# A residual update shared by two engines, and a first unit that multiplies rounded halves first

## The reference

```python
h = rms_norm(x, g_pre)          # x * rsqrt(mean(x*x) + 1e-6) * gain
m = branch(h)                   # starts with a product h @ W
x = x + rms_norm(m, g_post)     # in the second block 0.5 * for the two feed-forwards
```

## Time and profile before

| | |
|---|---|
| median of 3 runs | 3150.82 us (3149.11 to 3152.02) |
| the profiled execution | 3147.1 us, its span 3145.3 us |
| TensorE matmul busy | 2929.5 us, 93% of the span |
| TensorE weight load busy | 2289.0 us |
| VectorE busy | 1164.5 us |
| ScalarE busy | 1288.0 us |
| GpSimd busy | 1156.5 us |
| mean granted TensorE clock | 0.97 of full |

### The profile page before, as it was taken

One profiled execution on the slowest core, in us unless ns is written; L12 is line 12 of the kernel. 1 busy time (PEld: TensorE's weight loads), 2 busy tenths in 40 slices (PEclk: granted clock), 3 DMA queues, 4 the chain that ended last, 5 costly groups with the idle time before them and its releaser, 6 DMA issues.

```text
span 3145.3 us, 40673 instructions
## 1 busy us (share of the span) xinstructions
PE 2929.5 (93%) x14437; PEld 2289.0 (73%) x14437; DVE 1164.5 (37%) x1551; ACT 1288.0 (41%) x1707; POOL 1156.5 (37%) x256
## 2 busy tenths in 40 slices
PE   7998998999989989998999989999498999999997
PEld 5864686888768755886887768887296778678886
DVE  5154214555132362125553054430304531354422
ACT  5356443555235366434553233322224353333332
POOL 2410253344544200542445524455131325434453
PEclk9999998999999999999999989999699999999998
DMA  6210132233335100332332323322221213323322
GB/s 147 86 30 1 40 104 83 80 93 88 89 91 110 54 2 3 98 101 67 98 102 74 103 74 98 95 83 75 73 86 32 71 41 96 101 67 93 98 83 73
DMA packets 441756, 242.34 MB, mean 77 GB/s; under 512 B 39158, under 2 KB 440246, under 8 KB 441654
## 3 DMA queue, kind: packets, MB, share of 16 engines
q1 hardware_dynamic: 438320, 240.13, 27.6%
q10 hardware_dynamic: 3334, 0.85, 0.2%
HBM read 238.48 MB, written 2.70 MB: 77 GB/s over the span
## 4 chain that ended last, share of the span: by engine, by line
PE 60%; issue 27%; POOL 6%; DVE 3%; ACT 2%; DVEq 1%; SPq 1%; POOLq 0%; DMA 0%; ACTq 0%
PE pair L1459 54%; POOL wlo L454 6%; SPq L405 1%; PE pair L1641 1%; DVEq L970 1%; PE pair L1662 1%; DVE x L972 0%; ACT bP L775 0%; PE pair L1679 0%; PE pair L1721 0%; DVE nstat L1155 0%; DVE pair L968 0%; DVEq L973 0%; PE pair L1719 0%; PE pair L1877 0%
## 5 line engine op out<-in xcount | busy, mean ns | idle before, releaser
L454 POOL TENSOR_TENSOR wlo<-raw,whi 128x2048 fp32r<-128x2048 f32 x251 | 1156.2, 4606 | 1955.1 <-ACT whi L469 1955.1
L1459 PE MATMUL pair<-hh,whi 128*128 128x512 f32 (+1 forms) x2256 | 885.9, 393 | 35.4 <-DVE hl L944 23.0
L1459 PE MATMUL pair<-hl,whi 128*128 128x512 f32 (+1 forms) x2256 | 883.0, 391 | 0.0
L1459 PE MATMUL pair<-hh,wlo 128*128 128x512 f32 (+1 forms) x2256 | 882.8, 391 | 0.0
L469 ACT ACTIVATE whi<-raw 128x2048 fp32r<-128x2048 f32 x251 | 480.0, 1913 | 512.2 <-PE pair L1459 462.7
L1459 PEld LDWEIGHTS pair<-hh,whi 128*128 128x128 f32 (+1 forms) x2256 | 425.4, 189 | 135.8 <-DVE hl L944 22.8
L1459 PEld LDWEIGHTS pair<-hl,whi 128*128 128x128 f32 (+1 forms) x2256 | 425.5, 189 | 90.1
L1459 PEld LDWEIGHTS pair<-hh,wlo 128*128 128x128 f32 (+1 forms) x2256 | 425.0, 188 | 90.7
L1270 DVE TENSOR_TENSOR a2lo<-tmp,a2hi 128x512 f32 x44 | 200.0, 4546 | 79.5 <-ACT a2hi L760 79.5
L983 DVE COPY branch<-pair 128x512 f32 x32 | 22.1, 692 | 463.9 <-ACT sq L515 358.9
L1459 PE MATMUL pair<-a1hi,whi 128*128 128x512 f32 x352 | 139.7, 397 | 3.6 <-DVE a1lo L1248 3.6
(11 more groups left out here) (307 smaller groups left out, 3852.1 us busy)
## 6 DMA issues: line engine op xcount, KB each, us to landing
raw<-in_w_in SPq DMA_DIRECT2D x122, 512.0 KB, 4.1
raw<-in_w_up SPq DMA_DIRECT2D x88, 512.0 KB, 4.8
raw<-in_ffn_w_gate SPq DMA_DIRECT2D x44, 512.0 KB, 4.0
raw<-in_ffn_w_up SPq DMA_DIRECT2D x44, 512.0 KB, 5.2
raw<-in_w_out SPq DMA_DIRECT2D x24, 512.0 KB, 4.4
raw<-in_w_down SPq DMA_DIRECT2D x32, 384.0 KB, 3.6
raw<-in_ffn_w_down SPq DMA_DIRECT2D x32, 384.0 KB, 3.6
raw<-in_w_down SPq DMA_DIRECT2D x32, 320.0 KB, 4.0
```

What stands on the lines that cost most here:

```text
L454: pool.tensor_tensor(wlo[:, s, :], raw[:, s, :], whi[:, s, :].bitcast(f32), ALU.subtract).then_inc(lo_ready, 1)
L1459: o = pe.matmul(out, l, r, start=start and first, stop=stop and last)
```

## The change

Three things, in all handovers:

- **Residual update.** `post_norm` writes the normalised odd tile into `tmp` (SBUF) and the even one into PSUM. VectorE adds the even one to x, as a plain sum, and GpSimd adds the odd one (`odd_tiles`). The factor 0.5 is multiplied into the gains of norms 9 and 13 once, at the start. The semaphores are `t_odd`, `x_odd` and `x_even`; ScalarE squares the tiles in the order 1, 0, 3, 2, 5, 4, 7, 6.
- **Remainders.** In `pre_norm` odd tiles go to `tmp` too, and GpSimd makes their `hl` (`odd_remainders`); VectorE makes the even ones.
- **First unit.** A `ready` unit issues, for each k, whi x hh and wlo x hh for both banks after a wait for `hh`, then whi x hl for both banks after a wait for `hl`.

GpSimd's single loop over units is cut into loops with these pieces between them. SyncE waits for the eight sums of squares (`sq_used`) where it waited for `x_ready`. The first norm of the program keeps its form on VectorE.

```diff
+            def odd_tiles(j):
+                for c in range(4):
+                    pool.wait_ge(S.t_odd, 4 * j + c + 1)
+                    pool.tensor_tensor(x[:, 2 * c + 1], x[:, 2 * c + 1], tmp[:, c % 2], ALU.add).then_inc(S.x_odd, 1)
+            def odd_remainders(m):
+                for c in range(4):
+                    k = 2 * c + 1
+                    pool.wait_ge(S.hh_ready, KT * m + k + 1)
+                    pool.tensor_tensor(hl[:, k], tmp[:, c % 2], hh[:, k].bitcast(f32), ALU.subtract).then_inc(S.h_odd, 1)
...
+                rest(v0 + 16, 0)
+                odd_tiles(2 * l)
+                rest(v0 + 16, 1)
+                odd_remainders(2 * l + 1)
...
                 for k in range(KT):
-                    if k > 0:
+                    if k % 2 and k > 4:
+                        dve.wait_ge(S.h_odd, 4 * m + k // 2 - 1)
+                    dve.scalar_tensor_tensor(tmp[:, k // 2 % 2] if k % 2 else NORM[k // 2 % 2][:, :], x[:, k], gains[:, bass.ds(KT * n + k, 1)], RSTD[:, :],
+                                             ALU.mult, ALU.mult).then_inc(S.h_set, 1)
+                    if k % 2:
                         dve.drain()
-                    dve.scalar_tensor_tensor(NORM[k % 2][:, :], x[:, k], gains[:, bass.ds(KT * n + k, 1)], RSTD[:, :],
-                                             ALU.mult, ALU.mult).then_inc(S.h_set, 1)
-                    if k >= 1:
                         lower(k - 1)
-                lower(KT - 1)
...
-                for k0 in range(0, KT, 2):
-                    for k in (k0, k0 + 1):
-                        dve.scalar_tensor_tensor(NORM[k % 2][:, :], branch[:, k], gains[:, bass.ds(KT * n + k, 1)], RSTD[:, :],
-                                                 ALU.mult, ALU.mult)
+                def even(c):
+                    dve.tensor_tensor(x[:, 2 * c], NORM[c % 2][:, :], x[:, 2 * c], ALU.add).then_inc(S.x_even, 1)
+
+                for c in range(4):
+                    if c >= 2:
+                        dve.wait_ge(S.x_odd, 4 * j + c - 1)
+                    for k, to in ((2 * c + 1, tmp[:, c % 2]), (2 * c, NORM[c % 2][:, :])):
+                        o = dve.scalar_tensor_tensor(to, branch[:, k], gains[:, bass.ds(KT * n + k, 1)], RSTD[:, :], ALU.mult, ALU.mult)
+                        if k % 2 == 1:
+                            o.then_inc(S.t_odd, 1)
                     dve.drain()
-                    for k in (k0, k0 + 1):
-                        dve.scalar_tensor_tensor(x[:, k], NORM[k % 2][:, :], scale, x[:, k], ALU.mult, ALU.add).then_inc(S.x_ready, 1)
-                    dve.drain()
+                    even(c)
...
-                        ready(ki)
+                        ready[0](ki)
                         for b, _, c0 in tiles:
-                            wt = [w[s][:, k * width + c0:k * width + c0 + P] for w in (wh, wl)]
-                            o = three(bank[b][:, :], wt, [inp[0][:, ki], inp[1][:, ki]], j == 0, j == nk - 1)
+                            at = k * width + c0
+                            pe.matmul(bank[b][:, :], wh[s][:, at:at + P], inp[0][:, ki], start=j == 0, stop=False)
+                            pe.matmul(bank[b][:, :], wl[s][:, at:at + P], inp[0][:, ki], start=False, stop=False)
+                        ready[1](ki)
+                        for b, _, c0 in tiles:
+                            at = k * width + c0
+                            o = pe.matmul(bank[b][:, :], wh[s][:, at:at + P], inp[1][:, ki], start=False, stop=j == nk - 1)
```

More of the change, by code:

```diff
@@ L284, in build @@
             start_x gains_t gains_set tables_t tables_copied ang_ready sin_done tables_ready negones_set
-            x_ready sq_done sq_used sum_done rstd_done h_set hh_ready h_ready
+            x_ready x_even t_odd x_odd sq_done sq_used sum_done rstd_done h_set hh_ready h_even h_odd
             rs_ready rope_done k_exchanged cmp_in kvAB_ready v_ready v_ready_dve gateT_set gate_t gate_ready
@@ L371, in _ @@
                 unit(v0 + 2, 0, twin(W, 896, W, 1152, 0))
-                sp.wait_ge(S.x_ready, KT * (2 * l + 1))
+                sp.wait_ge(S.x_ready, KT)
+                sp.wait_ge(S.sq_used, KT * 4 * l + KT)
                 sp.wait_ge(S.tables_ready, 1)
@@ L485, in root, with pre_squares @@
                 act.activation(RSTD[:, :], RSTD[:, :], ACT.Exp, scale=-0.5).then_inc(S.rstd_done, 1)
[L487 to L492, removed]
+            def pre_squares(n, m, first=False):
+                for p in range(KT):
+                    k = p ^ 1
+                    if first:
+                        act.wait_ge(S.x_ready, k + 1)
+                    else:
+                        act.wait_ge((S.x_even, S.x_odd)[k % 2], 4 * (m - 1) + k // 2 + 1)
+                    if p >= 2:
+                        act.wait_ge(S.sq_used, KT * n + p - 1)
+                    act.activation(sq[:, p % 2], x[:, k], ACT.Square).then_inc(S.sq_done, 1)
                 root(n, True)
@@ L499, in pre_upper @@
                     act.wait_ge(S.h_set, KT * m + k + 1)
-                    act.activation(hh[:, k], NORM[k % 2][:, :], ACT.Copy).then_inc(S.hh_ready, 1)
+                    act.activation(hh[:, k], tmp[:, k // 2 % 2] if k % 2 and between is None else NORM[(k if between is not None else k // 2) % 2][:, :], ACT.Copy).then_inc(S.hh_ready, 1)
             def pre_norm(n, m):
@@ L1025, in _ @@
             dve.wait_ge(S.gains_t, 1)
-            dve.tensor_copy(gains[:, :], bank[6][:, 0:GAINS * KT]).then_inc(S.gains_set, 1)
+            dve.tensor_copy(gains[:, :], bank[6][:, 0:GAINS * KT])
+            dve.drain()
+            for n in (9, 13):
+                dve.tensor_scalar(gains[:, KT * n:KT * n + KT], gains[:, KT * n:KT * n + KT], 0.5, None, ALU.mult)
+            dve.drain().then_inc(S.gains_set, 1)
             dve.wait_ge(S.pos_in, 16)
@@ L1052, in _, with first_lower @@
             reduced(ang, 0.25, TWO_PI / 4)
-            pre_norm(0, 0)
+            dve.drain()
+            dve.wait_ge(S.rstd_done, 1)
+            def first_lower(k):
+                dve.wait_ge(S.hh_ready, k + 1)
+                dve.tensor_tensor(hl[:, k], NORM[k % 2][:, :], hh[:, k].bitcast(f32), ALU.subtract).then_inc((S.h_even, S.h_odd)[k % 2], 1)
+            for k in range(KT):
+                if k > 0:
+                    dve.drain()
+                dve.scalar_tensor_tensor(NORM[k % 2][:, :], x[:, k], gains[:, k:k + 1], RSTD[:, :], ALU.mult, ALU.mult).then_inc(S.h_set, 1)
+                if k >= 1:
+                    first_lower(k - 1)
+            first_lower(KT - 1)
             dve.wait_ge(S.sin_done, 2)
@@ L1759, in _ @@
                 for i in range(4):
-                    two_tiles(v0 + 14 + i // 2, i % 2, (yhi, ylo), (lambda k: pe.wait_ge(S.y_ready, 8 * l + k + 1)) if i == 0 else None)
+                    two_tiles(v0 + 14 + i // 2, i % 2, (yhi, ylo), y_tiles(8 * l) if i == 0 else None)
                 variance(4 * l + 1)
```

59 lines of the change are left out of this document (44 added, 15 removed).

## The result

| | before | after |
|---|---|---|
| median | 3150.34 us (4 runs, 3149.11 to 3152.02) | 3126.25 us (4 runs, 3122.07 to 3130.53) |
| ratio, with its 95% interval | | 0.9918, 0.9905 to 0.9931 |
| profiled execution, its span | 3147.1, 3145.3 us | 3122.07, 3120.3 us |
| GpSimd busy | 1156.5 us | 1222.2 us |

The kernel is 24 us faster by the medians, 25 by the two profiled executions, where I had predicted 18.1. Direction and places were right; the gain is larger than the forecast.

A forecast was written before the change was run, and what follows sets the result against it. TensorE was taken as the bound, standing still 3.9 us at each of six handovers. Squares 8.0 + first product 5.6 + clock 2 + end 2.9 - start 0.4 = 18.1 us off, giving 3132.7; own range 3128 to 3139, stretched to 3125 to 3142.

The forecast's parts named there:

- Squares, 8.0: Residual update in six handovers: x ready earlier, TensorE's squares end sooner without gaps; 8.0 us saved, bounds 5 and 10.
- First product, 5.6: After each handover's squares: TensorE starts on `hh` without waiting for `hl`; 0.93 us, six times, 5.6 us saved.
- GpSimd's piece, 1.2: One 512-column sum or subtraction on GpSimd in a handover takes 1.2 us.
- VectorE's pair, 2.15: Two tiles on VectorE in the residual update, two products and one sum, take 2.15 us.
- Two engines at SBUF, nothing: VectorE's new handover instructions have one SBUF and one PSUM tensor, so GpSimd does not hold them up; no cost.
- the slack that I gave the piece: Residual update: with d per GpSimd piece, last odd x comes at 0.8 + 4d, later than before from d = 2.7.
- Order of the halves, nothing: 47 units with new order and second wait per k keep pace 0.2265; no cost, upper bound 17.8 us.
- The clock, 2: Windows after the six handovers: shorter idle time gives back 2 us of 12.0 lost to lower clock; bounds -1 and 12.
- the clock stays up: Rival, behind the handovers: clock stays up after the shorter idle stretch, 10 us more, 3123; chance 0.06.
- End, 2.9: Kernel's end: the last tiles are transposed earlier, 2.9 us saved.
- Start, -0.4: Kernel's start: two tiny products and two drains before `gains_set`, four steps at 0.1, 0.4 us lost.
- its 3197 for a piece of 4.53 us: Rival "Slower", residual update: large fixed GpSimd cost, last odd x 7.2 later, seven times, some 3197; chance 0.03.

The follow-up runs named there:

- a second profile: The changed kernel run again with no edit, which gave a second profile; 3125.97 us, ratio 0.9924 to the kernel before.
- the order alone: Kernel before with only the first unit's new order and its two waits; update and remainders stay on VectorE; 3143.94 us, 0.9972.
- fill: Matmuls of a 128-column constant that keep TensorE busy, results overwritten; in both idle stretches of the changed kernel: 3124.52 us, 0.9917.
- fill_squares: Such filler matmuls in the idle time ahead of the squares; alone on the changed kernel 3121.7 us, with the start mended 3123.85 us.
- fill_product: Such filler matmuls between squares and first product; alone on the changed kernel 3128.93 us, on the kernel before 3151.95 us.

## Why the forecast was right, and where it fell short

**Squares, 8.0: right.** 7.9, 9.1 and 8.0 in the three profiles. TensorE ends this stretch, and it runs without gaps.

**First product, 5.6: right**, 5.3 with a second profile at 5.2; the order alone gives 5.3. TensorE does not run dry after it, and only because GpSimd helps: with VectorE alone it does, for 8.9 us.

**GpSimd's piece, 1.2: right**, 1.26 to 1.29; VectorE's pair, 2.15: 2.10. **Two engines at SBUF, nothing: right**; `a2lo` still takes 4544 ns, while `tmp` is written at 0.75 beside GpSimd. But the slack that I gave the piece was too large. I let it grow to 2.7 before it hurt, because I compared its last x with the last x of before, 11.73. At 2.7 it cost 16 us of the gain: the squares now end 2.8 behind the last odd x instead of 2.2, and what they must not exceed is TensorE's own end, 12.4, and no longer 13.9. With the last odd x at 0.9 + 4d, as measured (d is the time of one piece), my estimate for the limit is d = (12.4 - 2.8 - 0.9) / 4 = 2.2, hardly more than VectorE's pair. That the work went to the slower engine did not matter: each piece takes 1.26 against VectorE's 0.69, and the whole is faster, since it is TensorE that sets the end. The Trainium skill (GPSIMD Engine Reference, Engine selection) gives elementwise work to VectorE; the trace agrees on the pace, and the case shows where the advice stops.

**Order of the halves, nothing: right.** In the first unit of a feed-forward body of the changed kernel, TensorE's timeline has

```profile
562.53 0.39 PE L1546 MATMUL pair<-hh,whi 128*128 128x512 f32 x1
...
572.05 0.39 PE L1546 MATMUL pair<-hh,whi 128*128 128x512 f32 x1
```

with 42 matmuls from the one to the other: 9.52 / 42 = 0.2267, as before. And the order alone is faster, not slower.

**The clock, 2: the step that failed.** It gave back 7.3 in one profile, 8.6 in the other. I wrote that 2.9 lies between 0.99, which left the clock up, and 3.85, which brought it down, "nearer to the latter", and priced it with the idle time alone. I allowed up to 12 for it, but the forecast's own range, 3128 to 3139, took only the 2 us, and the measured median lies 2 us below it. The idle time alone does not tell what the clock does. With 2.9 to 3.2 us of it and no filler, it stayed up behind 17 of 36 handovers. A gap in the squares separates them better, 16 of 21 without and 1 of 15 with one, but not cleanly. What separates all 36 is how long before the end of the squares the clock had last risen. In the windows over the squares it can be worked out: where the clock rises once in a stretch, it was up for 2 x (PEclk - 0.5) x length at its end. The first three handovers of the changed kernel, then the first and the third of the order alone:

```profile
524.74:534.84 10.10, 10.10 (x16) 3.58 (x16) 5.41 (x9) 4.25 (x7) 8.28 (x4) 0.73 0.00 1
914.76:924.42 9.66, 9.66 (x16) 3.38 (x16) 5.41 (x9) 4.25 (x7) 7.91 (x4) 0.76 0.01 3
1418.03:1427.07 9.04, 9.04 (x16) 3.13 (x16) 5.41 (x9) 4.25 (x7) 7.28 (x4) 0.83 0.00 1
...
527.69:538.66 10.97, 9.19 (x16) 3.18 (x16) 8.11 (x12) 4.26 (x7) 3.35 (x1) 0.87 0.34 96
1426.15:1437.12 10.97, 10.24 (x16) 3.65 (x16) 8.11 (x12) 4.29 (x7) 3.36 (x1) 0.75 0.36 96
```

That gives 4.6, 5.0, 6.0, 8.1 and 5.5 us; the clock stayed up behind the second and the last of these five. Over all kernels without `fill`, by handovers:

| idle before the product | clock had risen 4.8 to 5.8 us before the squares' end: stayed up | earlier or later: stayed up |
|---|---|---|
| 2.9 to 3.2 us | 17 of 17 | 0 of 19 |
| 3.7 to 3.9 us | 0 of 4 | 0 of 8 |

So both halves of the change count. The order shortens the idle time. The shared update ends the squares sooner after the rise. The rise comes on average 4.1 us after the first sum of squares begins with the order alone, 4.5 and 4.0 in the two profiles of the changed kernel. But the last sum ends 10.6 to 11.0 us after that beginning with the order alone, and 9.0 to 10.1 in the changed kernel. So the end lies 5.5 to 8.1 us behind the rise in the one, 4.6 to 6.0 in the other. I take a gap for a mark of an early rise, behind which TensorE catches up with VectorE. The five handovers without a gap where the clock fell had 4.6, 6.0, 6.0, 6.0 and 4.4 us, and the one with a gap where it stayed up had 5.5. With `fill_squares` and no `fill_product` the clock was up all through the squares, with an idle time of 2.9 to 3.0, and it fell in 12 of 14. This is a pattern of these traces, found in them afterwards. No run moved the rise by itself, and why these distances matter stays open. That the clock holds most of what the forecast lacked is shown by the profiles.

The same stretch of squares, that of the first handover, took 10.11 in one profile and 9.02 in the other, so where the clock rises in it differs from one execution to the next. The Trainium skill (TensorE: Matmul & The Clock Gate, What's actually happening) says that the number of slow matmuls at a kernel's start varies from run to run of one kernel; here the trace shows the like in the middle of one. The rival "the clock stays up" (0.06, 10 us more than the 2) was thus more than half true, and it was given too little.

**End, 2.9: mis-sized**, 1.8. The last transposes moved from 10.9 to 8.5 behind `post_norm`, but the copies and stores behind them did not follow in full: 0.6 of it is gone at the span's end. **Start, -0.4: mis-sized**, -0.7; I had counted four steps at 0.1.

With the clock at 7.3 to 8.6, the end at 1.8 and the start at -0.7, the sum is 21.6 for the first profile and, with a start of -0.6, 24.1 for the second, against 25.0 and 22.1 between the spans. The rest, 3.4 and -2.0, has the sign of the clock ahead of the first handover (0.99 and 0.97 against 0.98), which the change does not touch. One slip in a rival: its 3197 for a piece of 4.53 us adds seven times 7.2 to the profiled execution; on the median it would have been 3201.

## What to carry over

When a change shortens an idle stretch of TensorE and moves the end of the work ahead of it, price the clock behind it at both levels, and give the better one real weight: here that term was worth more than the removed wait. For a helper engine that makes every second tile, count from its last piece to the end of the stage, with all the steps that follow it in the new order, and compare that with the end that the bound engine sets after the change. And where two halves of a change each gain alone, look in the profile for what only their combination does.

## What was not expected of the hardware

- The granted clock behind an idle time of 2.9 to 3.2 us depended on what lay before it: it stayed up in 17 of 17 handovers where it had risen 4.8 to 5.8 us before the squares' end, in none of the 19 others. Small matmuls of 128 columns in the idle time held it up behind 14 of the 16 handovers that had them in the changed kernel and its versions, the two others being the ones with the late product; on the kernel before, behind three of six.
- Behind a jump back in TensorE's program, 4.69 us of issue stood open once the jump came 2.3 us later.
- Two profiles of the same program reach the first handover 5.3 us apart (521.93 and 527.27), with a granted clock of 0.99 and 0.97 up to there, which is more than each of three of the five terms of the forecast. Terms of one or two us must be read from distances inside a handover, never from spans.
